# Products of 512 weight columns written as two of 256

## What is computed

```
z = u @ w_in                                          # (256, 2048) @ (2048, 11264)
...
merged = gate_a * (y_a @ w_branch_a) + gate_b * (y_b @ w_branch_b)
return merged @ w_out
...
h = h + mixer_block(rms_norm(h, norm_mix_w[l]), ...)
u = rms_norm(h, norm_mlp_w[l])
h = h + jnp.square(jax.nn.relu(u @ w_up[l])) @ w_down[l]
...
proj = jnp.einsum('bld,dc->blc', hn, w_in[layer])     # (272, 2048) @ (2048, 6656)
...
y = jnp.einsum('blc,cd->bld', jnp.concatenate([ya, yb], axis=-1), w_out[layer])
```

## Time and profile before

| | us |
|---|---|
| median of 3 runs | 1893.75 |
| lowest, highest | 1892.94, 1893.94 |
| span of the profiled execution | 1893.3 |
| PE busy in it | 1879.6 |
| VectorE busy | 1101.4 |
| ScalarE busy | 889.3 |
| GpSimd busy | 143.6 |

### The profile page before, as it was taken

How to read it: one execution, slowest core, us unless ns; L and a number is a source line. 1 busy time by engine, 2 the same in 40 slices (tenths; PEclk the granted TensorE clock), 3 DMA queues, 4 the chain that set the end, 5 groups by cost and what they waited for, 6 DMA issues and landing times.

```text
span 1893.3 us, 33876 instructions
## 1 busy us (share of the span) xinstructions
PE 1879.6 (99%) x13432; PEld 1743.7 (92%) x13432; DVE 1101.4 (58%) x1270; ACT 889.3 (47%) x1171; POOL 143.6 (8%) x122
## 2 busy tenths in 40 slices
PE   9999999999999999999999999999999999999998
PEld 9989998999999889988998899899889999899986
DVE  6556766667655555545445445445565556767664
ACT  6544444455544445443444344334454355664543
POOL 2001322411001100000010000000010000000000
PEclk9999999999999999999999999999999999999999
DMA  8566565566565656656665665566556655354454
GB/s 270 184 181 177 181 179 178 165 200 180 168 231 191 214 186 179 194 198 192 196 192 193 194 191 194 194 190 190 189 185 181 179 170 150 105 147 144 156 190 143
DMA packets 176434, 346.47 MB, mean 183 GB/s; under 512 B 10976, under 2 KB 11184, under 8 KB 175776
## 3 DMA queue, kind: packets, MB, share of 16 engines
q1 hardware_dynamic: 174176, 337.76, 57.2%
q0 software_dynamic: 2128, 6.82, 1.4%
HBM read 342.44 MB, written 2.10 MB: 182 GB/s over the span
## 4 chain that ended last, share of the span: by engine, by line
PE 97%; DVE 1%; ACT 0%; DMA 0%; issue 0%; SPq 0%; DVEq 0%; ACTq 0%
PE ps L446 58%; PE ps L458 33%; PE ps L548 1%; PE ps L781 1%; DVE wlo L1301 1%; PE ps L771 1%; PE ps L748 1%; PE ps L791 0%; DMA raw<-in_w_in_dram 0%; ACT whi L899 0%; PE ps L476 0%; PE ps L759 0%; PE ps L599 0%; PE ps L591 0%; DVE xlo L1323 0%; PE ps L610 0%
## 5 line engine op out<-in xcount | busy, mean ns | idle before, releaser
L1301 DVE TENSOR_TENSOR wlo<-raw,whi 128x1024 fp32r<-128x1024 f32 x631 | 796.5, 1268 | 698.1 <-ACT whi L899 697.1
L899 ACT ACTIVATE whi<-raw 128x1024 fp32r<-128x1024 f32 x631 | 664.5, 1058 | 886.3 <-PE ps L446 551.5
L446 PE MATMUL ps<-xhi,whi 128*128 128x256 f32 (+1 forms) x1904 | 542.2, 285 | 0.4 <-DVE wlo L1301 0.3
L446 PE MATMUL ps<-xhi,wlo 128*128 128x256 f32 (+1 forms) x1904 | 531.3, 279 | 0.0
L446 PE MATMUL ps<-xlo,whi 128*128 128x256 f32 x1664 | 462.5, 278 | 0.0
L446 PEld LDWEIGHTS ps<-xhi,whi 128*128 128x128 f32 x1904 | 359.1, 189 | 9.3 <-issue 6.7
L446 PEld LDWEIGHTS ps<-xhi,wlo 128*128 128x128 f32 x1904 | 357.8, 188 | 0.0
L446 PEld LDWEIGHTS ps<-xlo,whi 128*128 128x128 f32 x1664 | 313.4, 188 | 1.5 <-issue 0.7
L446 PE MATMUL ps<-x2hi,whi 128*128 128x256 f32 x1024 | 282.8, 276 | 0.0
L446 PE MATMUL ps<-x2hi,wlo 128*128 128x256 f32 x1024 | 282.7, 276 | 0.0
L446 PE MATMUL ps<-x2lo,whi 128*128 128x256 f32 x1024 | 282.7, 276 | 0.0
(11 more groups left out here) (373 smaller groups left out, 2370.6 us busy)
## 6 DMA issues: line engine op xcount, KB each, us to landing
raw<-in_w_in_dram SPq DMA_DIRECT2D x279, 512.0 KB, 3.8
raw<-in_w_up_dram SPq DMA_DIRECT2D x128, 512.0 KB, 3.7
raw<-in_w_down_dram SPq DMA_DIRECT2D x128, 512.0 KB, 3.7
raw<-in_w_out_dram SPq DMA_DIRECT2D x64, 512.0 KB, 3.8
raw<-in_w_branch_a_dram SPq DMA_DIRECT2D x16, 512.0 KB, 4.9
raw<-in_w_branch_b_dram SPq DMA_DIRECT2D x16, 512.0 KB, 3.8
x_nat<-in_x_dram SPq DMA_DIRECT2D x4, 512.0 KB, 7.4
rel<-in_rel_turned_dram POOLq DMA_DIRECT2D x8, 256.0 KB, 4.3
```

What stands on the lines that cost most here:

```text
L446: ins = mm(outs[b], w[:, k % SLOTS, j, cols], v, start=start, stop=last and j == CK - 1 and i == 2, skip_group_check=True)
L899: f(whi[:, k % SLOTS], raw[:, k % SLOTS], ACT.Copy).then_inc(whi_ready, 1)
L1301: tt(wlo[:, k % SLOTS], raw[:, k % SLOTS], whi[:, k % SLOTS], ALU.subtract).then_inc(wlo_ready, 1)
```

## The change

In `chunk_n` the 512 columns are taken as two halves. For each row block and each half of the tokens, the three products are made for columns 0 to 255 and then for 256 to 511, both into the same PSUM bank as before, at the same columns. The two lo products change places, so that the order of the three is that of `chunk_t`. The flag that begins a bank anew stands on the first product of the first half alone. Semaphores, slots and all other engines' programs are as before.

```diff
                     for t in halves:
                         toks = slice(t * P, (t + 1) * P)
-                        for i, (v, w) in enumerate(((xh, whi), (xh, wlo), (xl, whi))):
-                            ins = mm(ps[:, 2 * s + t, :], v[:, kt, toks], w[:, k % SLOTS, j, :],
-                                     start=first and j == 0 and i == 0,
-                                     stop=last and j == CK - 1 and i == 2, skip_group_check=True)
+                        for half in range(2):
+                            cols = slice(half * CW // 2, (half + 1) * CW // 2)
+                            for i, (v, w) in enumerate(((xh, whi), (xl, whi), (xh, wlo))):
+                                ins = mm(ps[:, 2 * s + t, cols], v[:, kt, toks], w[:, k % SLOTS, j, cols],
+                                         start=first and j == 0 and i == 0 and half == 0,
+                                         stop=last and j == CK - 1 and i == 2, skip_group_check=True)
```

## The result

| | before | changed |
|---|---|---|
| median, us | 1893.67 (4 runs) | 1911.36 (4 runs) |
| lowest, highest | 1892.94, 1893.94 | 1908.61, 1911.79 |
| profiled execution, span | 1893.3 | 1909.9 |
| ratio | | 1.0088, 95% interval 1.0076 to 1.0100 |

Forecast were 1888.0 us and a range of 1885 to 1906; the time is 17.7 us over the median of before.

The account below looks back on a forecast made before the run. PE's products were taken to bound the kernel; 2688 products of 512 columns split into 5376 at L446's 113.4 ns gave -5.7 us, other terms nothing: 1893.75 - 5.7 = 1888.0 us, range 1885 to 1906.

Parts of the forecast that it names:

- What bounds the kernel: Whole kernel: TensorE (PE) products make up 97% of the chain, 58% on L446 and 33% on L458.
- The gain per pair in the fast rhythm: chunk_n: two 256-column products at 113.4 ns take 2.1 ns less than one of 512; 0.82 us less for 384.
- The bound from above: New products' interval: L446's slower rhythm of 117.8 ns makes a pair 235.6 ns, 18.0 us more in all.
- Which rhythm: Split runs of chunk_n: entered from weight runs or behind L476 transposes, nearly all take the fast rhythm, 113.4 ns.
- if their rhythm changes behind the new groups: Runs of L446, code unchanged: should keep 87.07 us; otherwise the forecast's sum misses it. No size given.
- Side work: Transposes or score products between chunks in 9 places of chunk_n: costed at nothing, or 0.1 us a place (0.9 us).
- re-entry costs almost nothing: chunk_n behind the L476 transposes: 96 products follow in 21.99 us, 229.1 ns each, so resuming is nearly free.
- Feeding, order, instruction fetch: chunk_n: weights still arrive in time, the new order meets no wait, instruction fetch is 0.4% of DMA time; cost nothing.
- Rival 1: Split products: overhead belongs to each product, not its length; 116.1 ns each, +8.9 us, 1902.7 us; chance 0.13.
- Rival 2: Split products: slow rhythm throughout, 117.8 ns each, +18.0 us, 1911.8 us; chance 0.14.
- Rival 3: Split products: slow rhythm in part, behind side work, or a mixture; +4.4 us, 1898 us; chance 0.18.
- The range: Total time 1885 to 1906 us, holding forecast, rivals 1 and 5 and nearly all of 3, 0.8 together.

Follow-up runs that it names:

- e4: Changed kernel with the first and last block of each group and the first of chunk 2 left 512 columns wide: 1899.33 us, ratio 1.0023 to the kernel before.
- e6: Changed kernel with only the last block of three products of each group left at 512 columns: 1901.78 us, ratio 1.0033 to the kernel before.
- e7: Kernel before, in the new product order, with only the last chunk of w_down in quarters 1 to 3 split: 1903.25 us, ratio 1.0045.
- e2: Changed kernel with the three products back in the old order: 1908.19 us, ratio 1.0072 to the kernel before.
- e3: Changed kernel with both halves of a product next to each other on the same stationary block: 1910.90 us, ratio 1.0088 to the kernel before.
- e9: Changed kernel with the first and last block of each group and all of chunk 2 at 512 columns: 1896.33 us, ratio 1.0011 to the kernel before.
- e1: Kernel before, products kept at 512 columns, only the order of the three changed: 1895.58 us against 1895.37, ratio 1.0004.
- e5: Kernel before, new order, split only in w_down quarters 1 to 3 except groups' first and last blocks, and in the last projection: 1892.01 against 1894.25 us, ratio 0.9986.

## Why the prediction was wrong, point by point

- **What bounds the kernel**: right. PE's products in a row are 97% of the chain before and after.
- **The gain per pair in the fast rhythm**: right, to a tenth. Predicted were 0.82 us less for 384 products; 87.04 and 87.05 us against 87.89 and 87.91 are 0.85 and 0.86.
- **The bound from above**: right. 117.8 ns was read from L446 in the profile before, and the slow stretches of L460 have 90.45 / 768 = 117.8 ns.
- **"Which rhythm"**: the step that failed, in two places. The split products were forecast at 5.7 us less and took 8.6 us more, 14.3 us of the miss. First, the step took the fast stretches of the earlier trace rows as proof that a run entered from another weight run keeps the fast rhythm. One of its three rows was misread: the run of 936 is entered from side work (L610, L612, L509), not from a weight run. The other two, and every run of L446 in the MLP before but the one behind the transposes, were entered from products of 512 columns, and e4, e6 and e7 show that these are what hands the fast rhythm over. With them gone, the rhythm is kept from w_up into w_down (16 of 16 borders in the traces of the changed kernel, twice, e2 and e3) and turns over from w_down into w_up (12 of 12, and 3 of 3 in e7). Second, the transposes of L476 were likened to those of L599, which lead to fast stretches of L446. At this placing all six stretches of `chunk_n` behind L476 were slow, in every kernel that splits them but e9, and three of four behind the score products in the changed kernel.
- **Costed at nothing, and the second largest miss**: w_up. The prediction said once that the sum misses it "if their rhythm changes behind the new groups", but gave it no price in the forecast or in a rival; it was 6.6 us.
- **Side work**: wrong for what follows it. The eight transposes take 0.87 us as before, but "re-entry costs almost nothing" was read from wide products (229.1 ns). The split ones behind side work take 117.8 ns: 6.8 us in all over the fast rhythm, where the prediction had 0 or 0.9. These 6.8 us are part of the 14.3.
- **Feeding, order, instruction fetch**: right. The chain has no new wait, e1 shows the order at 1.0004, the queue of the instructions still has 0.4%, and PE takes twice the products at 113.3 ns.
- **Rival 1, an extra for each product**: refuted by the split runs at 87.04 us. So is the rule of the Trainium skill, TensorE: Matmul & The Clock Gate, "Back-to-back issue gap", as it was used: a further 2.5 ns for each product would have made the run of 768 longer than that of 384, and it is shorter. (The section gives this formula for a product by itself, and for a stream of loads and products 131 ns at 512 columns; 228.9 ns were measured.) That the total is on the rule's side of zero has another cause.
- **Rival 2, slow throughout, 1911.8 us**: its time came true by luck, its mechanism only in part. 3312 of the 5376 split products were slow, 62%; the rest of the loss came from L446.
- **Rival 3, slow in part, 1898 us**: this is what happened to the split products by themselves (+8.6 us by the table, 1902 us). It had the right mechanism, and stopped short of the neighbours.
- **The range** ended at 1906 because rival 2 was left out, and because no case let the slow rhythm spread to unchanged code.

What stays open: what in the hardware makes the two rhythms, and what sets one at a border. The MLP's pattern recurs in four traces (the changed kernel twice, e2, e3), so it isn't chance there, and the placing decides which rhythms there are. But why split products of w_down turn the rhythm over on the way into w_up, no run tells; those of w_out don't (144 products in 16.96 us, then 48 of L446 in 5.66 us, both in the slow rhythm, in the changed kernel). No run took the side work itself away, and none moved the weight slots.

## What to carry to other kernels

When PE bounds a kernel and its products follow without a wait, divide the length of unbroken runs by their counts, for every stage: two values for the same instruction mean a second rhythm, and a change of shape can move code between them that it doesn't touch. Before you change shapes or buffers, note which runs have which value, and after the change compare the runs of unchanged code first. A reshaping can then be kept only in those stages where its runs come out fast, as in e5.

## What was not expected of the hardware

- A stream of 256-column fp32r products, each with its load, has two steady intervals, 113.3 and 117.8 ns, at the same granted clock (0.999), with the same code and operand buffers. Each lasts for hundreds of products. In the MLP a run of w_down takes over the one of w_up ahead of it, and a run of w_up takes the other one than the split w_down ahead of it (e7: 36 split products are enough for that).
- Moving the activation buffers by 64 bytes in each partition, with nothing else changed, took the kernel before from 1894.93 to 1948.70 us: the interval of L446 went from 113.4 to 118.7 or 120.0 ns, that of the 512-column products from 228.9 to 232.3 or 233.3 ns.
- Products of 512 columns have a second interval as well, 233.3 ns, when they are entered from a slow stretch (e1, e7).
